# A decoder trunk on one core: sorting the tokens by expert group once per layer, and transposing the gated activation from every fourth column

## The reference

```python
h = rms_norm(x, norm_w).reshape(-1, D)
g_p, g_idx = lax.top_k(softmax(h @ wg + bg), 1)            # one of 4 groups
e_p, e_idx = lax.top_k(softmax(e_logits_of_that_group), 2) # two of its 4 experts
...
for e in range(N_EXPERTS):                                  # 16
    a = jax.nn.silu(h @ w_gate[e]) * (h @ w_up[e])          # 2048 -> 512
    y = y + combine[:, e:e + 1] * (a @ w_down[e])           # 512 -> 2048
return x + y
```

## Time and profile before

| | |
|---|---|
| median of 3 runs | 1746.99 us (1745.36 to 1749.21) |
| the profiled execution | 1747.63 us, span 1745.8 us |
| PE, PEld busy | 94%, 77% |
| DVE, ACT, POOL busy | 82%, 62%, 5% |
| moved from HBM | 470 MB, 271 GB/s over the span |
| a pass of the loop | 149.2 us |

### The profile page before, as it was taken

How to read it: one execution, slowest core, us unless ns; L and a number is a source line. 1 busy time by engine, 2 the same in 40 slices (tenths; PEclk the granted TensorE clock), 3 DMA queues, 4 the chain that set the end, 5 groups by cost and what they waited for, 6 DMA issues and landing times.

```text
span 1745.8 us, 22647 instructions
## 1 busy us (share of the span) xinstructions
PE 1637.6 (94%) x7933; PEld 1343.1 (77%) x7933; DVE 1432.2 (82%) x1625; ACT 1087.4 (62%) x1274; POOL 91.3 (5%) x71
## 2 busy tenths in 40 slices
PE   5999987987899999999999997799999999999998
PEld 4999873466688878878887885688877887887886
DVE  4476778865599899899989976679989989998996
ACT  4443433043477777677777764267777877777784
POOL 0000010000000020030011000000020003003000
PEclk9999998987899999999999998699999999999999
DMA  9654431442599789889979983269979988997991
GB/s 313 215 181 147 161 127 49 145 169 97 182 375 377 295 329 379 332 286 378 377 273 335 383 315 111 90 225 376 373 279 343 374 323 309 380 379 249 367 374 77
DMA packets 99917, 473.41 MB, mean 271 GB/s; under 512 B 18506, under 2 KB 21852, under 8 KB 49668
## 3 DMA queue, kind: packets, MB, share of 16 engines
q1 hardware_dynamic: 93508, 465.59, 72.4%
q10 hardware_dynamic: 6336, 6.88, 1.2%
HBM read 470.32 MB, written 2.11 MB: 271 GB/s over the span
## 4 chain that ended last, share of the span: by engine, by line
PE 76%; DVE 12%; issue 7%; ACT 3%; DMA 1%; ACTq 1%; POOL 0%; DVEq 0%; POOLq 0%
PE ps L1419 22%; PE ps L1421 21%; PE ps L1420 21%; DVE split_lo L937 6%; PE ps L1501 3%; PE ps L1681 3%; DVE cat L937 2%; DVE xn L933 2%; PE ps L1662 1%; PE ps L1385 1%; ACT split_hi L596 1%; PE ps L1530 1%; ACT xn L604 1%; ACT cat L596 1%; DVE work L1297 0%
## 5 line engine op out<-in xcount | busy, mean ns | idle before, releaser
L937 DVE TENSOR_TENSOR split_lo<-ring,split_hi 128x1024 fp32r<-128x1024 f32 x864 | 1082.5, 1273 | 163.0 <-ACT split_hi L596 117.4
L596 ACT ACTIVATE split_hi<-ring 128x1024 fp32r<-128x1024 f32 x864 | 909.6, 1059 | 329.4 <-PE ps L1421 310.8
L1419 PE MATMUL ps<-split_hi,cat 128*128 128x512 f32 (+1 forms) x1728 | 686.9, 398 | 23.0 <-DVE cat L937 14.1
L1421 PE MATMUL ps<-split_hi,cat 128*128 128x512 f32 (+1 forms) x1728 | 673.3, 390 | 0.0
L1420 PE MATMUL ps<-split_lo,cat 128*128 128x512 f32 (+1 forms) x1728 | 673.0, 389 | 0.0
L1419 PEld LDWEIGHTS ps<-split_hi,cat 128*128 128x128 f32 x1728 | 325.7, 188 | 117.8 <-DVE split_lo L937 31.6
L1421 PEld LDWEIGHTS ps<-split_hi,cat 128*128 128x128 f32 x1728 | 325.7, 188 | 68.2
L1420 PEld LDWEIGHTS ps<-split_lo,cat 128*128 128x128 f32 x1728 | 326.2, 189 | 63.6 <-issue 0.5
L584 POOL TENSOR_TENSOR x_sb<-work,x_sb 128x512 f32<-128x512 f32 x48 | 81.1, 1690 | 947.1 <-ACT work L596 947.1
L1419 PE MATMUL ps<-cat,split_hi 128*128 128x256 f32 x384 | 111.4, 290 | 5.1 <-DVE split_lo L937 5.1
L1420 PE MATMUL ps<-cat,split_hi 128*128 128x256 f32 x384 | 109.7, 286 | 0.0
(11 more groups left out here) (155 smaller groups left out, 693.4 us busy)
## 6 DMA issues: line engine op xcount, KB each, us to landing
ring<-in_w_gate SPq DMA_DIRECT2D x128, 1024.0 KB, 5.6
ring<-in_w_up SPq DMA_DIRECT2D x128, 1024.0 KB, 5.6
ring<-in_w_down SPq DMA_DIRECT2D x128, 1024.0 KB, 5.9
ring<-in_w_in_e SPq DMA_DIRECT2D x32, 1024.0 KB, 5.0
ring<-in_w_out_e SPq DMA_DIRECT2D x16, 1024.0 KB, 5.1
ring<-in_pool_w_o SPq DMA_DIRECT2D x4, 1024.0 KB, 8.3
x_sb<-in_x SPq DMA_DIRECT2D x2, 1024.0 KB, 7.1
ring<-in_w_in_e SPq DMA_DIRECT2D x8, 256.0 KB, 4.7
```

What stands on the lines that cost most here:

```text
L596: return nc.scalar.activation(out, in_, ACT.Copy, scale=scale)
L937: return tt(dst, full, hi.bitcast(F32), ALU.subtract)
L1419: mm(out, sh, mh, start=start, stop=False, **how)
L1421: return mm(out, sl, mh, start=False, stop=stop, **how)
```

## The change

1. **Sorted once.** Directly after routing, one gather of all 256 tokens in order of their groups: `pick` is now tokens by 256 slots, and 32 matmuls of 256 columns go to banks 0, 1 and 4 to 7. ACT copies the result over `xn` (`sorted_x`), and the first 128 slots also to `hgT[0]`. A pass no longer gathers: its tokens are 128 columns of `sorted_x` from a start that is loaded into a register (`window_i`), which ACT copies and DVE subtracts.
2. **Order.** The last up product stands ahead of the down products of experts 2 and 3 (`UNITS`). The copies for the next pass lie between the splits 84 to 95, and the next pass waits for them by pairs of units.
3. **Adding back.** `add_passes`, `stage` and ACT's copies are gone; DVE adds each scatter from PSUM to `x_sb` in every pass.
4. **Activation.** `times_up` writes in order; the transpositions read every fourth column. `actT` has two buffers.
5. **Routing.** The place in the sorted order needs the counts of the lower groups: 14 small matmuls, and some more small DVE operations.

```diff
-UNITS = [(0, "g"), (0, "u"), (1, "g"), (0, "d"), (1, "u"), (2, "g"), (1, "d"), (2, "u"), (3, "g"), (2, "d"),
-         (3, "u"), (3, "d")]
+UNITS = [(0, "g"), (0, "u"), (1, "g"), (0, "d"), (1, "u"), (2, "g"), (1, "d"), (2, "u"), (3, "g"), (3, "u"),
+         (2, "d"), (3, "d")]
-GATHER_BANK = (0, 1, 0, 1)
+GATHER_BANK = (0, 1, 4, 5, 6, 7, 4, 5)
+        sorted_x = xn[:].rearrange("p (k s) -> p k s", k=KC)
-        actT = cat_cut(2 * D, FC, P)
+        actT = [cat_cut(2 * D + i * 2 * FF, FC, P) for i in range(2)]
...
-                with pool.Fori(1, n) as p:
-                    for i in range(8):
-                        t, b = i // 4, i % 4
-                        pool.wait_ge(m["staged"], (p - 1) * 8 + (i + 1))
-                        cols = x_sb[:, t, b * 512:(b + 1) * 512]
-                        nc.gpsimd.tensor_tensor(cols, stage[:, i % STAGES, :], cols, ALU.add).then_inc(m["x_moved"], 1)
...
-                def slots_hi(p, q):
-
-                    act.wait_ge(m["gathered"], p * 4 + (q + 1))
-                    copy(hgT[0][:, 4 * q:4 * q + 4, :], ps[:, GATHER_BANK[q], :].rearrange("p (k s) -> p k s", k=4)) \
-                        .then_inc(m["slots_hi"], 1)
-
-                for q in range(4):
-                    slots_hi(0, q)
+                def slots_hi(p, q, w):
+
+                    if q == 0:
+                        unit_done(act, l, p - 1, EPG - 1, "u")
+                    copy(hgT[0][:, 4 * q:4 * q + 4, :], sorted_x[:, 4 * q:4 * q + 4, bass.ds(w, P)]).then_inc(m["slots_hi"], 1)
+
+                for i in range(8):
+                    act.wait_ge(m["gathered"], i + 1)
+                    two = slice(2 * i, 2 * i + 2)
+                    both = ps[:, GATHER_BANK[i], :].rearrange("p (k s) -> p k s", k=2)
+                    copy(sorted_x[:, two, :], both).then_inc(m["sorted_out"], 1)
+                    copy(hgT[0][:, two, :], both[:, :, 0:P]).then_inc(m["slots_hi"], 1)
...
+                    w = act.value_load(window_i[0:1, bass.ds(p + (l * NPASS + 1), 1)], min_val=0, max_val=P)
...
-                        if not first_pass and u - 3 in SCATTER_AT:
-                            i = SCATTER_AT.index(u - 3)
-                            act.wait_ge(m["scattered"], (p - 1) * 8 + (i + 1))
-                            if i == 0:
-                                act.wait_ge(m["x_moved"], (p - 1) * 8 + 1)
-                            if i >= STAGES:
-                                act.wait_ge(m["x_moved"], (p - 1) * 8 + (i - STAGES + 2))
-                            copy(stage[:, i % STAGES, :], ps[:, BANK_Y + i % 4, :]).then_inc(m["staged"], 1)
...
-                        by_j = lambda t: t.rearrange("p (j k) -> p j k", k=FC)
-                        stt(out=act.rearrange("p (k j) -> p j k", k=FC), in0=by_j(gated[:, e % 2, :]),
-                            scalar=comb_slot[:, e:e + 1], in1=by_j(ps[:, 2, :]), op0=ALU.mult, op1=ALU.mult) \
-                            .then_inc(m["act_done"], 1)
+                        stt(out=act, in0=gated[:, e % 2, :], scalar=comb_slot[:, e:e + 1], in1=ps[:, BANK_U, :],
+                            op0=ALU.mult, op1=ALU.mult).then_inc(m["act_done"], 1)
...
                         split(p, 4 + i, 5 + i)
+                        if not first_pass and i in SCATTER_AT:
+                            add_y(p - 1, SCATTER_AT.index(i))
...
-                    for q in range(3):
-                        slots_lo(p + 1, q)
+                    split(p, 84, 86)
+                    slots_lo(p + 1, 0, w)
+                    split(p, 86, 89)
                     turned_lo(EPG - 1)
-                    split(p, 92, 94)
-                    slots_lo(p + 1, 3)
-                    split(p, 94, 96)
+                    split(p, 89, 91)
+                    slots_lo(p + 1, 1, w)
+                    split(p, 91, 93)
+                    slots_lo(p + 1, 2, w)
+                    split(p, 93, 95)
+                    slots_lo(p + 1, 3, w)
+                    split(p, 95, 96)
...
-                gather(0)
+                pe.wait_ge(m["pick_ready"], 1)
+                for i in range(8):
+                    if i >= 6:
+                        pe.wait_ge(m["slots_hi"], i - 3)
+                    for k in (2 * i, 2 * i + 1):
+                        for t in range(NT):
+                            last = mm(ps[:, GATHER_BANK[i], (k % 2) * SEQ:(k % 2 + 1) * SEQ],
+                                      sorted_x[:, k, t * P:(t + 1) * P], pick[:, t, :], start=t == 0, stop=t == NT - 1)
+                    last.then_inc(m["gathered"], 1)
...
+                            if fresh and (first_pass or q % 2 == 0):
+                                pe.wait_ge(m["gather_out"], q + 1 if first_pass else p * 4 + (q // 2 + 5))
...
-                            last = turn(ps[:, BANK_T, k * P:(k + 1) * P], act[:, k * P:(k + 1) * P])
+                            last = turn(ps[:, BANK_T, k * P:(k + 1) * P], act.rearrange("p (j k) -> p k j", k=FC)[:, k, :])
...
-                            if e == EPG - 1:
-                                gather(p + 1, range(3))
-                                turn_act(e)
-                                gather(p + 1, range(3, 4))
+                        elif e == EPG - 2:
+                            down(e, lambda n: turn_act(EPG - 1) if n == 4 else None)
```

More of the change, by code:

```diff
@@ L262, in build @@
         cnt, o3 = cut(o3, NG)
+        lower, o3 = cut(o3, NT, NG)
+        late, o3 = cut(o3, NT, 1)
+        window, o3 = cut(o3, NPASS)
         assert o3 <= GAIN_AT
@@ L1210, in moe_dve @@
                 first_max(oneh, glog, col(0))
+                chain(tt(lower, prio.unsqueeze(1).to_broadcast([P, NT, NG]), gmax.to_broadcast([P, NT, NG]), ALU.is_lt))
                 tick_off().then_inc(m["rank_in"], 1)
@@ L1218, in moe_dve @@
                 dve.wait_ge(m["rank_done"], 1)
-                rank = ps[:, BANK_T, 0:16].rearrange("p (t c) -> p t c", t=NT)[:, :, 0:NG]
-                chain(stt(out=rank_in[:, :, 0:NG], in0=rank, scalar=1.0, in1=oneh, op0=ALU.add, op1=ALU.mult))
-                chain(ts(rank_in[:, :, NG:2 * NG], rank_in[:, :, 0:NG], -1.0 - P, None, ALU.add))
-                chain(ts(rank_in[:, :, 0:NG], rank_in[:, :, 0:NG], -1.0, None, ALU.add))
+                place = ps[:, BANK_T, 0:16].rearrange("p (t c) -> p t c", t=NT)[:, :, 0:NG]
+                chain(tt(t4b, place, oneh, ALU.mult))
+                chain(nc.vector.tensor_reduce(col(7), t4b, X, ALU.add))
+                for t in range(NT):
+                    last = ts(pick[:, t, :], slot_no, stat[:, 7, t:t + 1], None, ALU.is_equal)
+                last.then_inc(m["pick_ready"], 1)
+                rank = ps[:, BANK_T, 32:48].rearrange("p (t c) -> p t c", t=NT)[:, :, 0:NG]
+                chain(stt(out=t4a, in0=rank, scalar=float(P), in1=oneh, op0=ALU.is_ge, op1=ALU.mult))
+                chain(nc.vector.tensor_reduce(late, t4a, X, ALU.max))
+                nc.vector.memset(window[:, NG:], float(P))
+                chain(ts(window[:, 0:NG], ps[:, BANK_T, 24:24 + NG], float(P), None, ALU.min))
+                for t in range(NT):
+                    ts(rank_in[:, t, 0:NG], window[:, 0:NG], -1.0, stat[:, 7, t:t + 1], ALU.mult, ALU.add)
+                ts(rank_in[:, :, NG:2 * NG], col(7).to_broadcast([P, NT, NG]), -float(P), None, ALU.add)
                 nc.vector.memset(rank_in[:, :, 2 * NG:], -1.0)
-                for t in range(NT):
-                    last = ts(pick[:, t, :], slot_no, rank_in[:, t, 0:1], None, ALU.is_equal)
-                last.then_inc(m["pick_ready"], 1)
+                chain(nc.vector.tensor_copy(window_i[:, l * NPASS:(l + 1) * NPASS], window))
                 first_max(sel1, el, col(3))
@@ L1279, in add_y @@
                     tt(cols, ps[:, BANK_Y + b, :], cols, ALU.add).then_inc(m["x_moved"], 1)
[L1281 to L1282 removed]
+                for i in range(8):
+                    dve.wait_ge(m["slots_hi"], i + 1)
+                    two = slice(2 * i, 2 * i + 2)
+                    low(hgT[1][:, two, :], sorted_x[:, two, 0:P], hgT[0][:, two, :]).then_inc(m["gather_out"], 1)
                 def one_pass(p, first_pass=False):
+                    w = dve.value_load(window_i[0:1, bass.ds(p + (l * NPASS + 1), 1)], min_val=0, max_val=P)
                     def gate(e):
@@ L1311, in one_pass @@
                         split(p, 4 + i, 5 + i)
+                        if not first_pass and i in SCATTER_AT:
+                            add_y(p - 1, SCATTER_AT.index(i))
                         if i == 8:
                             gate(0)
-                    split(p, 16, 20)
+                    for u in range(16, 20):
+                        split(p, u, u + 1)
+                        if not first_pass and u - 4 in SCATTER_AT:
+                            add_y(p - 1, SCATTER_AT.index(u - 4))
                     times_up(0)
@@ L1673, in gather @@
-                def gather(p, quads=range(4)):
-                    pe.wait_ge(m["pick_ready"], p + 1)
```

(25 more changed lines are left out.)

91 lines of the change are left out of this document (42 added, 49 removed).

## The result

The changed kernel takes 1685.05 us in the median of 4 runs (1683.11 to 1687.65), the kernel before beside it 1747.0 (1745.36 to 1749.21): a ratio of 0.9646, with a 95% interval of 0.9628 to 0.9663. That is 62 us less, where 44.6 were forecast, and just under the low end of the range, 1686.

A forecast was written before the change was run, and what follows sets the result against it. PE was taken to bound each pass, working without pause, with a serial part at each layer's start. -62.0 - 10.2 + 6.7 + 11.6 + 9.3 = -44.6 gave 1702 us; range for 8 in 10: 1686 to 1724.

The forecast's parts named there:

- I take 1.7 of the 4 as given back in each of 6 loop passes: Around a loop pass's scatters, 1.7 of some 4 us of waits and operand changes saved: -10.2 us, bounds 0 and -24.
- The strided transpositions: Transpositions reading every fourth column cost 0.07 us more each, 96 times: +6.7 us, bounds 0 and 14.
- four transpositions in 0.6 to 0.75 us: Sign in the changed profile: an expert's four transpositions take this long on PE in place of 0.44 us.
- The gather: Gather taken out of each of 8 passes, worth 7.75 us of PE each: -62.0 us.
- The down products of experts 2 and 3 hide them: At a pass's end, 16 down units (21.8 us) cover the copies of the next pass's tokens.
- The start of the layers: Ahead of the first pass, longer ranks and gather of all 256 slots: +11.6 us in layer 0, +9.3 in layer 1.
- the wait behind layer 0's first units: PE's 5.98 us wait for ScalarE after four units of layer 0 stays; ScalarE is later by +1.0 us.
- DVE's busy time: DVE needs 126.5 us per pass against PE's 140; as a sign, under 130 us a pass.
- DVE falls behind around the pass boundary: Rival: DVE late around units 84 to 95 and the next start, 3 us a pass: 1726 us; chance 0.12.
- the clock stays at half: Rival: half clock through the long first gather, 11.3 us more a layer: 1725 us; chance 0.08.
- DMA becomes the bound: Rival: at only 352 GB/s a pass takes 142.9 us, 2.3 more in each of 8: 1720 us; chance 0.06.
- more than forecast: Rival: transpositions free and all waits around the scatters gone: 1685 us; chance 0.08.

The follow-up runs named there:

- e1: Kernel before, with only the adding back changed: DVE adds from PSUM, GpSimd's additions and ScalarE's copies to the stage gone; 1728.65 us, ratio 0.9903.
- e4: Changed kernel plus eight idle GpSimd additions in each loop pass, on tiles nobody else touches; 1711.96 us, ratio 0.9801.
- e12: Changed kernel plus eight unused DVE additions in each loop pass, early, one behind each addition of the scatters; 1711.21 us, ratio 0.9789.
- e13: Changed kernel plus eight unused DVE additions in each loop pass, late, behind splits 30 to 76; 1685.41 us, ratio 0.9633.
- e2: Changed kernel with the activation as before: DVE writes it in permuted order, transpositions read in order; 1685.76 us, ratio 0.965.
- e3: Changed kernel with the old order of the last three units (down 2, up 3, down 3); 1744.89 us, ratio 0.9986.
- e10: Changed kernel with five rank matmuls, gain and band loads inside the first pass, and GpSimd issuing the next router's four loads; 1666.74 us, ratio 0.9542.
- e7: Changed kernel with ScalarE's six loads of layer 0 issued inside the first pass instead of all ahead of it; 1682.66 us, ratio 0.9628.

## Why the prediction was off, point by point

The direction, the parts and their order of size were right; the gain was put at 44.6 us and was 62.

- **The step that failed: "How much of that reaches PE? ... I take 1.7 of the 4 as given back in each of 6 loop passes."** Measured 2.9 (e1), 7.2 us in all. I had nearly the right numbers for DVE (each addition of GpSimd costs it 1.1 us, measured 0.95; the moved ones make it 4 us shorter in a pass, measured 3.0), and then didn't use them, because "in a pass PE works without pause, ... DVE 136 us" of 149; the 1.7 comes from no row. The 136 is an average over the pass. In the 28 us from the first scatter DVE is busy 27.0, and what it gains or loses there reaches PE nearly in full (2.9 of 3.0 in e1, 4.4 of 4.7 in e4, 4.3 of 4.5 in e12), while elsewhere 3.2 us more of it (134.2 in e13, after 131.0) cost nothing. A stretch table of 28 us in place of 149 would have shown it, by the number of matmuls done, as the three of 10 us above do.
- **The strided transpositions, +6.7 us**, were mis-sized: measured 0.04 us for four, 1.2 us in all, and e2 finds no difference. The price was borrowed from DVE's strided normalisation, another engine's operand. The sign named for it, four transpositions in 0.6 to 0.75 us, didn't show either: 860.06 - 859.67 = 0.39. The Trainium skill's rule of lines (SBUF — State Buffer, Door 1: The DMA port swizzle), for which I dropped the lower bound of nothing, gives no size, and here 0.01 us a load is all that is seen.
- **The gather, -62.0 us**, is right and a little low: about 8.1 us each for 7.75. What the 0.4 us are wasn't tried.
- **"The down products of experts 2 and 3 hide them"**, of the copies at the end of a pass: right. PE's only waits in a loop pass, 0.6 us, are those for the halves of y. That the new order by itself is worth 60 us (e3) stands nowhere in the prediction, which counts the gather's 62 us without asking what the gather covered.
- **The start of the layers**, +20.9, measured +19.3: the ranks (+3.9) and the gather (+6.1 and +6.2) to a few tenths. The gather's first 4.5 us at half clock and the rest at full held as well, about: it took 15.97 us of the 16.2. That the wait behind layer 0's first units "stays" was right, and it grew by 2.3 us.
- **DVE's busy time,** put at 126.5 us a pass and under 130 as a sign, is 131.0; at that it still keeps up. No split takes over 1.3 us, as said.
- **The rivals.** "DVE falls behind around the pass boundary", "the clock stays at half" and "DMA becomes the bound" didn't come about. The rival "more than forecast", 1685 with a chance of 0.08, is what was measured, and mainly for its own two reasons: they give 12.7 us of the 17.4 that were missing, where the rival had 16.7. That the number fits to the microsecond is luck, made up by the gather, the start and the spread ahead of the router. It deserved more: the first reason had only a row of another engine against it, and the second followed from my own count of DVE.

## What to carry to other kernels

When an engine is the bound on the average of a loop, cut the loop into stretches a fifth as long and count the instructions that the bound engine completes in each; where another engine is busy in all of one, time added or removed there counts in full, however much it has to spare elsewhere. Before taking work out of a full engine, look what wait it stood in: taken out by itself it may give nothing (e3 against e1). An engine that a change leaves idle can take the issues that hold a busy one (e10).

## What had not been expected of the hardware

- A pause of 4.6 us on PE (3.06 and 1.49, with four transpositions between) was followed by 5.4 us at a granted clock of 0.50, 2.7 us lost on top of the wait; filled with idle matmuls it stayed at 1.00. Behind one of 4.75 us in e7 it was 0.50 from 480.9 to 484.0.
- Addition on GpSimd beside a split of two SBUF operands: one split took 2.18 us in place of 1.23. Over a pass the mean split takes 1.302 us in the kernel before, 1.273 in e4 and 1.223 in e1 and the changed kernel; for 96 splits that is 7.6 and 4.8 us more, so 0.95 and 0.6 us for each of eight additions. What decides between the two was not found.
- The issue of one small transfer to 128 partitions took ScalarE 5.7 to 7.0 us, behind another small one and with the DMA share at 1.0, and GpSimd 0.59 at a share of 0.18. Whether the engine or the moment decides was not tried.
